# Output projection of a hybrid decoder layer: a Strassen part over all row tiles, two products accumulated on others, and sixteen weight sums moved to an early stage

## The reference

```python
h = rms_norm(x, norm_g)
proj = jnp.einsum('bsd,de->bse', h, w_in)          # split into q, k, v, gate of three head groups
...
mixed = jnp.concatenate([
    out_a.astype(h.dtype) * jax.nn.silu(az),       # dilated window attention, 768 columns
    out_b.astype(h.dtype) * jax.nn.silu(bz),       # forgetting attention, 512 columns
    out_c.astype(h.dtype) * jax.nn.silu(cz)], axis=-1)   # gated linear attention, 768 columns
return x + jnp.einsum('bse,ed->bsd', mixed, w_out)       # (1024 x 2048) @ (2048 x 2048)
```

## Time and profile before

| what | value |
|---|---|
| median of 3 runs | 2040.43 us (2038.71 to 2040.92) |
| profiled execution, its own time | 2044.43 us |
| its span in the trace | 2042.7 us |
| TensorE busy (10024 matmuls) | 2008.2 us, 98% |
| VectorE / ScalarE / GpSimd busy | 55% / 44% / 25% |
| TensorE clock granted, mean | 0.998 of full speed |
| HBM read / written | 173.35 MB / 48.78 MB |

### The profile page before, as it was taken

How to read it: one execution, slowest core, us unless ns; L and a number is a source line. 1 busy time by engine, 2 the same in 40 slices (tenths; PEclk the granted TensorE clock), 3 DMA queues, 4 the chain that set the end, 5 groups by cost and what they waited for, 6 DMA issues and landing times.

```text
span 2042.7 us, 28729 instructions
## 1 busy us (share of the span) xinstructions
PE 2008.2 (98%) x10024; PEld 1690.6 (83%) x10024; DVE 1121.9 (55%) x1733; ACT 891.1 (44%) x1504; POOL 503.1 (25%) x400
## 2 busy tenths in 40 slices
PE   6999999999999999999999999999999999999998
PEld 5788888888888888888888888888888887788787
DVE  7611456465445555555555555555555657613797
ACT  7311343444454445445454445445444556411242
POOL 0000343251531212222221212222122210002565
PEclk9999999999999999999999999999999999999999
DMA  7322424324332222222222222323232274466646
GB/s 236 81 72 71 116 68 109 100 82 103 94 98 78 61 85 78 87 67 72 87 72 85 64 89 79 107 58 98 83 97 71 85 249 145 134 200 222 237 155 196
DMA packets 204559, 223.20 MB, mean 109 GB/s; under 512 B 17336, under 2 KB 143336, under 8 KB 203328
## 3 DMA queue, kind: packets, MB, share of 16 engines
q1 hardware_dynamic: 187760, 191.73, 31.8%
q10 hardware_dynamic: 16720, 30.45, 4.0%
HBM read 173.35 MB, written 48.78 MB: 109 GB/s over the span
## 4 chain that ended last, share of the span: by engine, by line
PE 85%; DVE 7%; ACT 2%; DMA 2%; issue 2%; POOL 1%; SPq 0%; DVEq 0%; ACTq 0%; POOLq 0%
PE acc L2266 19%; PE acc L2268 19%; PE acc L2267 19%; PE pv L2504 4%; PE turned L2489 4%; PE scores L2481 2%; PE scores L2478 2%; DVE w_lo L1724 1%; DVE act_lo L2209 1%; DMA w_raw<-in_w_in_dram 1%; PE acc L2616 1%; DVE fast_out L2222 1%; PE acc L2553 1%; PE acc L2555 1%; PE acc L2554 1%
## 5 line engine op out<-in xcount | busy, mean ns | idle before, releaser
L2266 PE MATMUL acc<-act_hi,w_hi 128*128 128x512 f32 x1848 | 737.1, 399 | 2.5 <-DVE w_lo L1724 1.9
L2268 PE MATMUL acc<-act_hi,w_lo 128*128 128x512 f32 x1848 | 722.0, 391 | 0.0
L2267 PE MATMUL acc<-act_lo,w_hi 128*128 128x512 f32 x1848 | 720.7, 390 | 0.0
L2268 PEld LDWEIGHTS acc<-act_hi,w_lo 128*128 128x128 f32 x1848 | 346.9, 188 | 75.4
L2266 PEld LDWEIGHTS acc<-act_hi,w_hi 128*128 128x128 f32 x1848 | 347.5, 188 | 69.5 <-DVE w_lo L1724 4.8
L2267 PEld LDWEIGHTS acc<-act_lo,w_hi 128*128 128x128 f32 x1848 | 347.7, 188 | 65.2
L1724 DVE TENSOR_TENSOR w_lo<-w_raw,w_hi 128x512 fp32r<-128x512 f32 x223 | 199.4, 894 | 358.6 <-ACT w_hi L1239 358.3
L1545 ACT ACTIVATE prob<-prob,neg_max 128x128 f32<-128x128 f32 (+7 forms) x160 | 124.0, 775 | 251.1 <-DVE neg_max L2035 251.1
L1159 POOL TENSOR_TENSOR vz<-raw 32x512 f32<-32x512 f32 x72 | 85.6, 1189 | 468.3 <-ACT sq L1492 465.6
L1239 ACT ACTIVATE w_hi<-w_raw 128x512 fp32r<-128x512 f32 x223 | 139.1, 624 | 137.2 <-PE acc L2268 110.1
L2051 DVE TENSOR_TENSOR pt_lo<-turned,pt_hi 128x1024 fp32r<-128x1024 f32 (+1 forms) x120 | 114.9, 957 | 146.9 <-ACT pt_hi L1553 146.3
(11 more groups left out here) (427 smaller groups left out, 3007.0 us busy)
## 6 DMA issues: line engine op xcount, KB each, us to landing
w_raw<-in_w_in_dram SPq DMA_DIRECT2D x240, 256.0 KB, 2.9
proj_scratch<-stage ACTq DMA_DIRECT2D x116, 256.0 KB, 2.1
w_raw<-in_w_out_dram SPq DMA_DIRECT2D x64, 256.0 KB, 3.5
raw<-proj_scratch SPq DMA_DIRECT2D x20, 512.0 KB, 3.4
logit_bias<-in_w_out_dram SPq DMA_DIRECT2D x35, 256.0 KB, 4.6
act_lo<-mixed_scratch SPq DMA_DIRECT2D x7, 1024.0 KB, 8.6
t_raw<-in_w_out_dram SPq DMA_DIRECT2D x28, 256.0 KB, 3.7
extra_raw<-in_w_out_dram SPq DMA_DIRECT2D x23, 256.0 KB, 3.5
```

Source lines behind the costliest of these rows:

```text
L2266: pe.matmul(acc, hi, xh, start=first, stop=False)
L2267: pe.matmul(acc, hi, xl, start=False, stop=False)
L2268: mm = pe.matmul(acc, lo, xh, start=False, stop=end)
```

## The change

**Row lists and runs.** `FAST_ROWS` now has two lists of eight row tiles, tiles 8 and 9 among them, so a product has eight items. One leftover is left, tile 9 for column group 0, and it stands first in `FAST_RUNS`. The products stand in another order; for products 2 and 6 (counted from 0) TensorE goes on in the banks of products 0 and 4 without clearing them (`FAST_ON_TOP`: `start` is false), so that their results are already summed there. `FAST_INTO` has 48 merges with the leftover's eight, where it had 72. `merges_at` spreads a run's merges over six items (`MERGE_STEPS`). In the last stage there are 696 matmuls instead of 708.

**Places.** `merged_into` swaps `res` and `fast_out[0]`: the partial result of column group 0 is loaded into `fast_out[0]` early, the residual of column group 2 into `res` later. Rows of pairs 8 and 9 are now stored to `mixed_scratch`: pair 8's at n == 7 of the early quarters (SyncE waits for it before the gate load at n == 10), pair 9's behind the sixth output quarter of column group 1, with a wait for it right behind.

**Weight sums sooner.** The 16 weight sums of products 1 and 2 are made in the stage without heads. SyncE loads two 128x512 tiles of `w_out` into halves of `g_wide` (`load_sooner`, two sets of buffers), GpSimd adds, SyncE stores the sum (`store_sooner`) in `summed_scratch`, one sum per quarter of the input weights. In the last stage these items load one tile from there. GpSimd makes its level masks for the heads behind these sums.

```diff
-FAST_ROWS = (list(range(7)), [7] + list(range(LAST + 1, KT)))
-FAST_LEFT = (LAST - 1, LAST)
+FAST_ROWS = (list(range(LAST - 1)), [LAST - 1] + list(range(LAST + 1, KT)) + [LAST])
...
+FAST_ON_TOP = (2, 6)
+SUMMED_SOONER = (1, 2)
+SOONER = [(q, j) for q in SUMMED_SOONER for j in range(FAST_K)]
+SOONER_AT = 2
+FAST_INTO = (((1, 0, ALU.add),), ((0, 1, ALU.add), (0, 0, ALU.add)), ((1, 1, ALU.add),),
+             ((0, 1, ALU.add), (1, 1, ALU.subtract)), ((1, 1, ALU.add),), ((1, 0, ALU.add), (0, 0, ALU.subtract)),
+             ((0, 0, ALU.add),))
-FAST_RUNS = [("product", 0), ("product", 1), ("left", 0), ("left", 1), ("left", 2)] + [("product", q) for q in range(2, 7)]
+FAST_RUNS = [("left", 2)] + [("product", q) for q in range(7)]
...
-ROW_SUM_STEP = [first + j for first in (9, 16, 23, 30, 37) for j in range(FAST_K)]
+MERGE_STEPS = 6
+ROW_SUM_STEP = [first + j for first in (4, 12, 20, 28, 36) for j in range(FAST_K)]
...
-            out += own[2 * (n - e - 1):2 * (n - e)]
+            out += [own[i] for i in range(len(own)) if e + 1 + i * MERGE_STEPS // len(own) == n]
...
+        sooner = [[g_wide[:, (2 * i + e) * HALF:(2 * i + e + 1) * HALF] for e in range(2)] for i in range(2)]
...
-        merged_into = [fast_out[0], fast_out[1], res]
+        merged_into = [res, fast_out[1], fast_out[0]]
...
-            with sp.Fori(AHEAD, C_ALONE) as s:
-                for kq in range(4):
-                    load_quarter(s, kq, COL_CQ + s * P)
+            def load_sooner(i):
+
+                if i == 0:
+                    sp.wait_ge(x_turned, 4 * NT)
+                elif i >= 2:
+                    sp.wait_ge(small_saved, 16 * i)
+                for to, (k, col) in zip(sooner[i % 2], weight_terms(*SOONER[i])):
+                    sp.dma_start(to, w_out_k[:, k, col:col + HALF]).then_inc(row_summed, 16)
+
+            def store_sooner(i):
+                sp.wait_ge(t_summed, i + 1)
+                sp.dma_start(summed[i * P:(i + 1) * P, :], sooner[i % 2][0]).then_inc(small_saved, 16)
+
+            for n in range(4 * (C_ALONE - AHEAD)):
+                load_quarter(AHEAD + n // 4, n % 4, COL_CQ + (AHEAD + n // 4) * P)
+                if 0 <= n - SOONER_AT - 1 < len(SOONER):
+                    store_sooner(n - SOONER_AT - 1)
+                if 0 <= n - SOONER_AT < len(SOONER):
+                    load_sooner(n - SOONER_AT)
...
+                if n == 7:
+                    store_pair(LAST - 1)
                 if n == 10:
                     sp.wait_ge(mix_lo, mixed_by(KK_GATED, 1))
+                    sp.wait_ge(mixed_saved, 16 * LAST)
                     load_gate(LAST, last_column)
...
+            sp.wait_ge(o_done, LAST + 3)
+            sp.dma_start(mixed[LAST * P:(LAST + 1) * P, :], vz[:]).then_inc(mixed_saved, 16)
             sp.wait_ge(mix_lo, MIX_ALL)
+            sp.wait_ge(mixed_saved, 16 * PAIRS)
             load_res(1)
...
+                kind, q = FAST_RUNS[run_of(n)[0]]
+                if kind == "product" and q in SUMMED_SOONER:
+                    i = SOONER.index((q, run_of(n)[1]))
+                    sp.dma_start(t_ones[slot], summed[i * P:(i + 1) * P, :]).then_inc(terms_in[slot], 16)
+                else:
+                    for to, (k, col) in zip((t_ones[slot], t_twos[slot]), weight_loads(n)):
+                        sp.dma_start(to, w_out_k[:, k, col:col + HALF]).then_inc(terms_in[slot], 16)
...
+            for i, (q, _j) in enumerate(SOONER):
+                pool.wait_ge(row_summed, 32 * (i + 1))
+                pool.tensor_tensor(sooner[i % 2][0], sooner[i % 2][0], sooner[i % 2][1], FAST_WEIGHTS[q][1]).then_inc(t_summed, 1)
...
+                on_top = kind == "product" and q in FAST_ON_TOP
...
-                    pe.matmul(banks[b], hi, t_his[slot], start=first, stop=False)
+                    pe.matmul(banks[b], hi, t_his[slot], start=first and not on_top, stop=False,
+                              skip_group_check=on_top)
```

More of the change, by code:

```diff
@@ L175, in weight_loads, with weight_terms @@
         return [(LEFT_ROWS[q][j], LEFT_COLS[q])]
+    return weight_terms(q, j)[:1 if q in SUMMED_SOONER else 2]
+def weight_terms(q, j):
     one, op, two = FAST_WEIGHTS[q]
@@ L182, in weight_op @@
     kind, q = FAST_RUNS[run_of(n)[0]]
-    return FAST_WEIGHTS[q][1] if kind == "product" else None
+    return FAST_WEIGHTS[q][1] if kind == "product" and q not in SUMMED_SOONER else None
 def weights_landed(n):
@@ L712, in _ @@
                 load_half_quarter(3, kq)
-            with sp.Fori(AHEAD, C_ALONE) as s:
-                for kq in range(4):
-                    load_quarter(s, kq, COL_CQ + s * P)
+            def load_sooner(i):
[14 more added lines that the diff above has]
+                    load_sooner(n - SOONER_AT)
+            for i in range(4 * (C_ALONE - AHEAD) - SOONER_AT - 1, len(SOONER)):
+                store_sooner(i)
+            sp.wait_ge(small_saved, 16 * (len(SOONER) + 1))
             def store_head(c):
@@ L1035, in _ @@
                 if 8 <= n < 8 + FAST_K:
-                    load_rows_again(1, 0, n - 8)
+                    load_rows_again(1, 1, n - 8)
                 if 14 <= n < 18:
                     for t in range(2 * (n - 14), 2 * (n - 14) + 2):
-                        load_partial(t)
+                        load_first_residual(t)
                 if 18 <= n < 18 + FAST_K:
                     load_rows_again(0, 1, n - 18)
-                if 28 <= n < 32:
-                    for t in range(2 * (n - 28), 2 * (n - 28) + 2):
+                if 20 <= n < 24:
+                    for t in range(2 * (n - 20), 2 * (n - 20) + 2):
                         save_merged(2, t)
-                if 45 <= n < 49:
-                    save_merged(0, 4 + n - 45)
+                if 48 <= n < 52:
+                    save_merged(0, 4 + n - 48)
             for t in range(4):
@@ L2615, in fast_item @@
                     hi, lo = (a[:, k, b * P:(b + 1) * P] for a in (act_hi, act_lo))
-                    pe.matmul(banks[b], hi, t_his[slot], start=first, stop=False)
-                    pe.matmul(banks[b], hi, t_los[slot], start=False, stop=False)
-                    mm = pe.matmul(banks[b], lo, t_his[slot], start=False, stop=at_end)
+                    pe.matmul(banks[b], hi, t_his[slot], start=first and not on_top, stop=False,
+                              skip_group_check=on_top)
+                    pe.matmul(banks[b], hi, t_los[slot], start=False, stop=False, skip_group_check=on_top)
+                    mm = pe.matmul(banks[b], lo, t_his[slot], start=False, stop=at_end, skip_group_check=on_top)
                     if at_end:
```

68 lines of the change are left out of this document (38 added, 30 removed).

## The result

Over 13 runs each, the changed kernel takes 2045.16 us (2044.1 to 2047.5) and the kernel before 2040.09 us (2038.7 to 2042.23): a ratio of 1.0026, with a 95% interval of 1.0018 to 1.0033. The change costs 5.1 us. The forecast was 2039.8 us, no measurable change; the time lies in the range, on the side of rival (b), and the interval leaves out no change.

The account below looks back on a forecast made before the run. TensorE, busy 2008.2 of 2042.7 us, was taken as the bound. Last stage -5.0 us, stage without heads +4.4, new row stores nothing: -0.6 us, from 2040.43 to 2039.8 us, range 2034.5 to 2047.5.

Parts of the forecast that it names:

- rival (b): Stage without heads: SyncE's turn is slower, 7.0 us, TensorE stalls 13.4 us from about 150 us on, 2048.8 us; chance 0.20.
- Last stage, -5.0 us: Last stage: 2.75 us from 12 fewer matmuls, 2.1 from two merge waits, 0.15 from a halved small wait.
- the merge waits: Last stage: two TensorE waits for merges at the start of leftover runs; both go, a gain of 2.1 us.
- The sums were covered before too, and I give them no gain: Last stage: weight sums already lay under other work, so their leaving it gives no gain.
- New row stores, 0: Stores of pairs 8 and 9: their waits, about 4 us for pair 9's, stay hidden, with a microsecond or two to spare.
- Stage without heads, +4.4 us: From about 100 us: SyncE's turn of 6.4 us exceeds the quarters' 5.44, so TensorE stalls 4.4 us.
- P: SyncE's turn in the stage without heads: time from the first load's issue to the sum's start, taken as 4.27 + 0.4 us.
- The limit of 6.11 us: Stage without heads: TensorE stalls 15 (c - 6.11) us, c being SyncE's turn; nothing below 6.1.
- I add nothing for the clock: Stage without heads: TensorE's waits come in pieces of 1 us or less, which never lowered the granted clock; cost nothing.
- the rule: Skill's 2.0 us per transfer and 436 GB/s: loads in after 3.2 us, turn 4.9, sum -5.0 us; not adopted.
- Rival (c): Last stage: lead not full when eight double-sum items begin, 6.0 us lost before the fifth product, 2045.8 us; chance 0.05.
- The decision point: Stage without heads: a SyncE turn of 6.7 us, where the stall is 9 us, divides no measurable change from slower.

## Why the prediction was wrong

- **Last stage, -5.0 us: right.** 5.45 us against the first profile of before, 5.1 against the second, 5.2 between medians. 2.75 for 12 matmuls as counted, the merge waits gone, the eight leftover merges behind the residual sums without a wait, accumulating on banks for nothing.
- **"The sums were covered before too, and I give them no gain": misleading.** True of the kernel before. With eight-item products and row sums from the fifth item on, leaving them in line costs 9.6 us. The forecast needed only that they were gone, so no term of the sum was hurt, but I did not see what the early stage was paying for.
- **New row stores, 0: right.** SyncE's waits in the changed kernel have 3.9 us for pair 9's store, where I said 4, and the quarter behind it, issued at 1814.53, is still split when TensorE frees its place and not when it lands:

```profile
SPq L987 <- DMA mixed_scratch<-vz: 3.9, 1, 3.9
1820.84 0.63 ACT L1320 ACTIVATE w_hi<-w_raw 128x512 fp32r<-128x512 f32 x1 [4.81 <-PE side L2651]
```

- **Stage without heads, +4.4 us: the step that failed.** The mechanism was right, place and shape: SyncE's turn, longer than 5.44 us, lateness that grows per turn, a slack, then TensorE waiting. The mis-sized term is P, "4.27 + 0.4": the mean was 5.0 us, so the turn was 6.74 us and not 6.4, and the stage cost 10.3 us in the trace and 10.0 between medians, not 4.4. Without a store ahead a pair took 4.25 us, with one 4.7 to 4.8 in the typical turn: both parts nearly as put. But I built the turn from one quiet pair, and three pairs in the stage met the two stores of a column group and took 5.6 to 6.0 us. Over the sixteen pairs the time above 4.67 us adds up to 5.7 us: 3.6 in these three, 1.2 in the first two, 0.9 in the other eleven. So 15 turns make 0.33 us into 5. The point against (b), that its slow pairs lay in a busy stretch, fell with the change itself: it raised the DMA share from 0.26 to 0.62.
- **The limit of 6.11 us: it fits, with some luck in the last digits.** The runs with turns of 5.86 us and less lost nothing. With the measured turn, 15 x (6.74 - 6.11) = 9.4, plus 0.9 for a first full pair at 102.23 instead of 101.3, the sum gives the 10.3 us of the trace. But it was made for the quarter of n = 18, and the last wait was for the one before it, issued at 189.83 behind the slow pair of 188.85: it left TensorE 9.7 us late. The quarter of n = 18 was split from 201.81 us on, which with 1.3 us for the splits is 9.5 us late. The clock and the restart made 9.7 into 11.5, and the 1.2 us of before the stage come off again.
- **"I add nothing for the clock", waits "in pieces of 1 us or less": wrong, and the second term that failed.** The two long waits were 2.5 and 2.6 us, and behind each the clock fell. The first fall was taken in by the next waits, the second cost 1.6 us in the profiled execution.
- **By the rule** that both loads are in after 3.2 us, an estimate ("DMA: Bandwidth & Descriptors" of the Trainium skill, Anatomy of one DMA) the stage would have been free. That section gives its figures for transfers issued by GpSimd, which the prediction did not say, and these are SyncE's. The trace disagrees with them here: 4.25 us for a pair without a store ahead, 5.0 on the mean beside the stage's other transfers.
- **Rival (c)** has the nearest number, 2045.8 us, and is wrong all the same: no wait of TensorE stands in the changed kernel's last stage.
- **Chances.** The decision point between no change and slower was put at a turn of 6.7 us, and the turn was 6.74. A term with a slope of 15 deserved a wider middle: 0.33 us of doubt about P is 5 us.

## What to carry to other kernels

When work is put into idle engines beside a stream of loads, write down the turn of the queue that issues both: every wait in it adds up, whatever is idle. Here one exchange of two steps (issue the next loads, then wait for the last result and store it) took the sum out of the turn and was worth 9.8 us, which put the changed kernel 5 us under the kernel before. Size such a turn by its mean over all that shares the queues, not by a quiet instance, and count how much lateness the reader has before it waits: the first 8 turns cost nothing, the later ones 1.2 to 1.4 us each, their full excess.

## What the runs showed of the hardware

While TensorE still had waits for a supply ahead, a lower granted clock (0.50 from 172 to 174 us) cost nothing: it restarted behind the last wait 9.7 us late with that fall and 10.1 late in a run without one. Behind the last wait a fall counted in full, 1.6 us for 3.7 us of slower matmuls. Waits of 2.3 to 2.8 us were followed by a fall in four cases (two in the changed kernel, one with 12 sums, one in the first profile of before) and a wait of 2.7 us by none in another run. A pair of 256 KB loads, from its first issue to the instruction that waits for both, took 4.25 us without a store ahead, 4.7 to 4.8 behind a 256 KB store of the same queue, and 4.9 to 6.1 where two 256 KB stores of another engine were issued within about 1.3 us of it; the last is a reading of places, not a test.
